# Fourteen pairs of gate-stage tiles by seven block products, convolution sums in PSUM, and low parts and weight sums on GpSimd

## The chip, the cores and the metric

The kernel runs on one core of one Trainium2 chip. The metric is the device time of one execution in microseconds (us). Engines are named as in the profile: PE is TensorE, DVE is VectorE, ACT is ScalarE, POOL is GpSimd, SP is SyncE, which issues most DMAs. On this kernel a difference of 0.2% (2.3 us) is about what a measurement tells from no change.

## The reference

One decoder layer over 1024 tokens and 1024 channels, float32 throughout.

```python
h = rmsnorm(x, ln_pre)                                  # (1024, 1024)
z = h @ w_in                                            # nine column groups
c_val, c_glu, c_gate, q, k, v, a_gate, g_conv, g_attn = split_columns(z)   # 1024 wide each, k and v 128
u  = c_val * sigmoid(c_glu)
c  = causal_depthwise_conv(u, w_dw, 31 taps) + b_dw
ya = (silu(layernorm(c)) @ w_pw * silu(c_gate)) @ w_br_conv
yb = (sliding_window_attention(q, k, v, sinks) * silu(a_gate)) @ w_br_attn
m  = sigmoid(g_conv) * ya + sigmoid(g_attn) * yb
x  = x + rmsnorm(m @ w_out, ln_post)
x  = x + sigmoid(x @ w_ple_gate) * (p @ w_ple_proj)
```

## The kernel before

Everything is kept transposed: 128 channels on the partitions, 1024 tokens along the free axis. A **tile** is 128 output channels for all 1024 tokens. It is 48 matmuls of 128x512: eight blocks of input channels, two halves of the tokens, and three passes, because a float32 product is made from values split in a rounded high part and the remainder: high x high, low weight x high input, high weight x low input. The rounded parts (`_hi`) are made by ACT, the remainders (`_lo`) by DVE, for the input once and for each tile's weights in turn (`high`, L1089, and `low`, L1558). The weights have two slots; a tile's weights can be split only when the tile two before it is done. PSUM has two slots of 1024 columns for tiles (`psg`) and four banks of 512 columns more (`psb`).

The program is one written-out order on each engine, tied by semaphores. It begins with the projection of `p` (eight short tiles), while DVE and ACT norm and split `h`. Then come 32 **gate-stage tiles** (`A0` to 31), four per round: GLU gate, value, `g_conv`, `g_attn` of the same 128 channels. `first_pair` (L653) holds the first two, `pairs(A0 + 2, Q0, ...)` the other thirty and the tiles of k and v. ACT turns each gate into tanh (`glu_and_merge`) and sends two of them to memory, DVE multiplies value and gate into `u` (L1711). Beside it DVE runs the convolution: `conv_steps` gives out the 31 taps of a row of 128 channels one by one, alternating between two sums, `conv` and `work`, both in SBUF (L1738). `tile_low(t + 1); taps(7)` or `taps(8)` fixes how many go between two weight splits. Eight q tiles follow, with the rest of the taps and the rotary turn (`rope`) on DVE; then attention beside eight tiles, and the later stages.

Two later stages (`seventh`, L1013) already use **seven block products** (Strassen's scheme, in Winograd's form): two tiles, four input-channel blocks apart by rows of the result, are made from seven products of half size instead of eight. A product is 12 matmuls. It needs sums of weight blocks, which POOL's DMAs add up in memory early in the run (`w_sums`), and sums of input blocks. Some products are added onto another product's PSUM bank, after ACT has copied the bank out (`keep`, L1376); those copies are combined by DVE (`take`). There the order of a pair's products is `P1, P2, P6, Q5, P7, Q3, P4`.

What touches the angles of the rotary turn: DVE makes them (L1687 to L1699), ACT takes two sines (L1180, L1181), POOL finishes cosine and sine (L1064 to L1067), all during the first gate-stage tiles.

Of the kernel before, what the change touches and what calls it, by code (L numbers as in the profile page):

```python
# [17 lines left out]
F32 = mybir.dt.float32  # L18
# [31 lines left out]
A0 = 0  # L50
K_TILE, V_TILE = 32, 33
Q0 = 34
C0 = 42
D0 = 50
E0 = 58
H0 = 66
I0 = 82
TILES = 98
WTILES = 82
# [34 lines left out]
def build(nc, dram):  # L94
    with ExitStack() as ctx:
# [22 lines left out]
        u_size = (4 * (PAD + S) + 31) // 32 * 32  # L118
        u = [at(f"u{j}", [PAD + S], F32, RD + 32 * KB - u_size * (2 - j)) for j in range(2)]
# [23 lines left out]
        block_raw = at("block_raw", [7, HALF], F32, GB + 24 * KB - 192)  # L143
        s_lo = at("s_lo", [4, KP, HALF], F32R, RD)
# [51 lines left out]
        v_last = cols[:, COL_TAPS:COL_TAPS + P]  # L196
# [85 lines left out]
        end_done = sem("end_done")  # L282
        merged_spilled = [sem("merged_spilled0"), sem("merged_spilled1")]
# [25 lines left out]
        banks01 = psb[:, 0:2, :].rearrange("p b s -> p (b s)")  # L309

# [153 lines left out]

        lower_rows = (4, 5, 6, 7, 0, 1, 2, 3)
# [9 lines left out]
        def _(sp):  # L475
# [29 lines left out]
            sp.dma_start(k_raw[:].bitcast(I32), POS).then_inc(pos_loaded, 16)  # L505
# [26 lines left out]

            sp.wait_ge(ps_free[0], K_TILE // 2 + 5)
# [26 lines left out]
            def load_block(b):  # L560
# [57 lines left out]
        def _(pe):  # L618
# [167 lines left out]

            first_pair()
            pairs(A0 + 2, Q0, h_hi, h_lo)

            def turn_values(k):  # L790

                if k != 1:
                    return
                pe.wait_ge(ps_free[1], 4 + V_TILE // 2 + 1)
                for c in range(NB):
                    mm = nc.tensor.transpose(psb[:, 2 + c // 4, (c % 4) * P:(c % 4 + 1) * P], v_t[:, c * P:(c + 1) * P], ident[:])
                mm.then_inc(v_turned, 1)

            tile(Q0 // 2, 0, h_hi, h_lo)
            tile(Q0 // 2, 1, h_hi, h_lo, beside=turn_values)  # L800
            pairs(Q0 + 2, C0, h_hi, h_lo)

            def scores(p, jp):
# [3 lines left out]
                if p == 0 and jp == 0:  # L807
                    pe.wait_ge(k_dup, 128)
# [234 lines left out]
        def _(pool):  # L1043
# [15 lines left out]
            pool.wait_ge(w_hi_ready, PLE_STEPS + 2)  # L1059
# [1265 lines left out]
```

## Time and profile before

| | |
|---|---|
| median of 3 runs | 1146.57 us (1145.72 to 1146.73) |
| the profiled execution | 1147.26 us |
| its span | 1145.5 us, mean granted clock 0.999 |
| PE busy | 1139.3 us (99%) |
| DVE busy | 925.0 us (81%) |
| ACT busy | 421.8 us (37%) |
| POOL busy | 29.8 us (3%) |

The busy time of PE is no measure of its pace: a matmul of 128x512 shows 390 ns, but the next one starts before it has ended. The pace is read from the chain, from the time of a run of matmuls and their count. Busy shares of DVE are averages over stages; it is fullest in the stretch of the gate-stage tiles.

### The profile page before, as it was taken

Reading aid. Unit: us, or ns where it says so; the run is one execution under the profiler, and the core shown is the slowest. Engines: PE = TensorE matmul, PEld = TensorE weight load, DVE = VectorE, ACT = ScalarE, POOL = GpSimd, SP = SyncE. Lnnn points to the kernel's source line nnn. Section 1 sums busy time; section 2 is a strip of 40 time slices with the busy share of each in tenths; the row PEclk is TensorE's granted clock in tenths of the full one; section 3 lists DMA queues with packets and bytes.
Section 4 is the critical chain, followed back from the end, with each engine's and each line's share of the span. In section 5 each row is a group of like instructions: output and inputs, shape, how many; then the busy total and the mean of one; then the engine's idle time right before and its main releaser. Section 6 shows DMA issues by size and latency. Waiting matters only on the chain.

```text
span 1145.5 us, 16085 instructions
## 1 busy us (share of the span) xinstructions
PE 1139.3 (99%) x6208; PEld 927.8 (81%) x6208; DVE 925.0 (81%) x1087; ACT 421.8 (37%) x763; POOL 29.8 (3%) x32
## 2 busy tenths in 40 slices
PE   9999999999999999999999999999999999999998
PEld 7788888888888888877777788888888888888887
DVE  5999999999999977489888589768767967557776
ACT  6422212212112121266666343332536435444342
POOL 2012010000000000000000000000000000000000
PEclk9999999999999999999999999999999999999999
DMA  9726787421221322411111211346553753334565
GB/s 350 286 92 179 206 238 201 111 92 55 73 86 50 111 51 65 101 38 57 57 57 57 74 49 44 92 135 205 166 173 120 252 182 127 115 117 141 182 200 184
DMA packets 46053, 148.00 MB, mean 129 GB/s; under 512 B 5648, under 2 KB 6416, under 8 KB 43952
## 3 DMA queue, kind: packets, MB, share of 16 engines
q1 hardware_dynamic: 32176, 92.77, 25.5%
q10 hardware_dynamic: 11520, 37.75, 9.5%
q0 software_dynamic: 2304, 16.78, 6.1%
q8 instruction: 32, 0.52, 0.2%
q14 instruction: 21, 0.17, 0.0%
HBM read 119.37 MB, written 41.94 MB: 141 GB/s over the span
## 4 chain that ended last, share of the span: by engine, by line
PE 92%; DMA 3%; DVE 3%; ACT 1%; SPq 1%; issue 1%; DVEq 0%; ACTq 0%
PE psg L629 66%; PE psb L1013 10%; PE psg L921 6%; DMA conv<-xT 2%; PE psb L835 1%; PE psg L892 1%; PE psg L1013 1%; PE psg L682 1%; PE psg L966 1%; PE psg L853 1%; ACT probs L1237 1%; PE psg L887 1%; PE psg L653 1%; PE psg L1037 1%; SPq L496 0%
## 5 line engine op out<-in xcount | busy, mean ns | idle before, releaser
L629 PE MATMUL psg<-h_hi,w_hi 128*128 128x512 f32 x768 | 236.8, 390 | 0.0
L629 PE MATMUL psg<-h_lo,w_hi 128*128 128x512 f32 x768 | 236.5, 389 | 0.0
L629 PE MATMUL psg<-h_hi,w_lo 128*128 128x512 f32 x768 | 236.4, 389 | 0.0
L1561 DVE TENSOR_TENSOR w_lo<-w_raw,w_hi 128x1024 fp32r<-128x1024 f32 x96 | 117.5, 1224 | 86.9 <-ACT w_hi L1093 83.4
L629 PEld LDWEIGHTS psg<-h_hi,w_hi 128*128 128x128 f32 x768 | 143.8, 188 | 30.5 <-issue 0.8
L629 PEld LDWEIGHTS psg<-h_lo,w_hi 128*128 128x128 f32 x768 | 144.1, 188 | 30.0
L629 PEld LDWEIGHTS psg<-h_hi,w_lo 128*128 128x128 f32 x768 | 144.1, 188 | 29.9
L1738 DVE SCALAR_TENSOR_TENSOR conv<-u,cols,conv 128x1024 f32<-128x1024 f32 x120 | 154.3, 1286 | 0.0
L1738 DVE SCALAR_TENSOR_TENSOR work<-u,cols,work 128x1024 f32<-128x1024 f32 x112 | 145.8, 1301 | 0.0
L1093 ACT ACTIVATE w_hi<-w_raw 128x1024 fp32r<-128x1024 f32 x95 | 100.5, 1057 | 103.8 <-PE psg L629 86.4
L1013 PE MATMUL psb<-s_hi,pair_w 128*128 128x512 f32 x240 | 73.9, 389 | 0.0
L1013 PEld LDWEIGHTS psb<-s_hi,pair_w 128*128 128x128 f32 x240 | 45.0, 188 | 9.4
L1994 DVE TENSOR_TENSOR pair_w<-block_raw,pair_w 128x512 fp32r<-128x512 f32 x56 | 37.9, 686 | 17.6 <-ACT pair_w L1354 17.6
L921 PE MATMUL psg<-h_hi,w_hi 128*128 128x512 f32 x128 | 51.8, 405 | 0.0
L921 PE MATMUL psg<-h_hi,w_lo 128*128 128x512 f32 x128 | 49.9, 390 | 0.0
L921 PE MATMUL psg<-h_lo,w_hi 128*128 128x512 f32 x128 | 49.9, 390 | 0.0
L1354 ACT ACTIVATE pair_w<-block_raw 128x512 fp32r<-128x512 f32 x56 | 34.5, 626 | 41.4 <-PE psb L1013 24.5
L1013 PE MATMUL psb<-s_lo,pair_w 128*128 128x512 f32 x120 | 46.7, 389 | 0.0
L629 PE MATMUL psg<-x_hi,w_hi 128*128 128x512 f32 x120 | 46.7, 389 | 0.0
L629 PE MATMUL psg<-x_hi,w_lo 128*128 128x512 f32 x120 | 46.7, 389 | 0.0
L629 PE MATMUL psg<-x_lo,w_hi 128*128 128x512 f32 x120 | 46.7, 389 | 0.0
L1013 PE MATMUL psb<-c_hi,pair_w 128*128 128x512 f32 x144 | 44.5, 390 | 0.2 <-DVE c_lo L2072 0.2
(305 smaller groups left out, 1817.5 us busy)
## 6 DMA issues: line engine op xcount, KB each, us to landing
w_raw<-weights SPq DMA_DIRECT2D x97, 512.0 KB, 3.6
gates<-ring ACTq DMA_DIRECT2D x24, 512.0 KB, 2.7
w_sums<-w_pairs POOLq DMA_DIRECT2D x12, 1024.0 KB, 7.8
ring<-gates ACTq DMA_DIRECT2D x24, 512.0 KB, 4.4
block_raw<-w_sums SPq DMA_DIRECT2D x32, 256.0 KB, 3.1
block_raw<-w_pairs SPq DMA_DIRECT2D x24, 256.0 KB, 4.6
x_rows<-x_rows SPq DMA_DIRECT2D x8, 512.0 KB, 10.7
conv<-xT SPq DMA_DIRECT2D x8, 512.0 KB, 14.9
```

The lines of the kernel that those rows point to most:

```text
L629: mm = nc.tensor.matmul(psg[:, slot, h * HALF:(h + 1) * HALF], w[:, wslot, (wk + k) * P:(wk + k + 1) * P], r[:, k, h * HALF:(h + 1) * HALF ...
L653: mm = nc.tensor.matmul(psg[:, slot, h * HALF:(h + 1) * HALF], w[:, slot, k * P:(k + 1) * P], r[:, k, h * HALF:(h + 1) * HALF], start=(k = ...
L682: mm = nc.tensor.matmul(psg[:, slot, cols_h], w[:, slot, k * P:(k + 1) * P], r[:, k, cols_h], start=(k == 0 and n == 0), stop=(k == KT - 1 ...
L835: mm = nc.tensor.matmul(psb[out_rows, 2 * jp + par, j2 * 2 * P + first:j2 * 2 * P + first + width], qo[rows, 4 * g + 2 * jp + j2, queries] ...
L853: mm = nc.tensor.transpose(psg_banks[:, bank, first + h * HD:first + h * HD + HD], probs[g][queries, 4 * jp + h, :], ident[queries, queries])
L921: mm = nc.tensor.matmul(gate_bank(p), w[:, t % 2, k * P:(k + 1) * P], r[:, k, half], start=(k == 0 and m == 0), stop=(k == KT - 1 and m == 2))
L1013: mm = nc.tensor.matmul(bank, pair_w[:, at_w, w, k * P:(k + 1) * P], r[:, k, :], start=(not onto and k == 0 and m == 0), stop=(k == KP - 1 ...
L1093: nc.scalar.activation(w_hi[:, j % 2, :], w_raw[:, j % 2, :], ACT.Copy).then_inc(w_hi_ready, 1)
L1354: nc.scalar.activation(pair_w[:, pair_slot(b), 0, :], block_raw[:, b % 7, :], ACT.Copy).then_inc(pair_hi, 1)
L1561: nc.vector.tensor_tensor(w_lo[:, slot, :], w_raw[:, slot, :], w_hi[:, slot, :].bitcast(F32), ALU.subtract).then_inc(w_lo_ready, 1)
L1738: own.step(stt(dst, src[:, j:j + S], tap(j), dst, ALU.mult, ALU.add))
L1994: nc.vector.tensor_tensor(pair_w[:, at_w, 1, :], block_raw[:, b % 7, :], pair_w[:, at_w, 0, :].bitcast(F32), ALU.subtract).then_inc(pair_l ...
```

## The change

Of the 32 gate-stage tiles only four are left as tiles (GLU and value of channel blocks 0 and 4). The other 28 are made as 14 pairs by seven block products (`EARLY`), in the order `ORDER`, in which P6 and P7 stand next to each other. Their sums of weight blocks are made in SBUF by POOL (four per pair, `early_sum`), and so are the seven low parts (`early_low`). POOL also takes over the low parts of the tiles 1 to 3, k, v and q, the sums for the convolution's mean (`add_to_mean`) and the angles of the rotary turn, now after the gate stage. The sums of the input blocks are made by DVE out of `h` before the third tile (`early_row_sum`, `early_row_low`), their high parts by ACT. The convolution works on input rows that lie in place in `conv`; its two sums lie in `psb`, and for the last row in SBUF (`last_sums`). The additions in memory for the two later stages (`w_sums`) move from POOL's first 200 us to behind the q tiles.

```diff
+ORDER = (P1, P2, Q5, P6, P7, Q3, P4)
+EARLY = [(GLU, 1), (VAL, 1), (GCONV, 0), (GCONV, 1), (GLU, 2), (VAL, 2), (GCONV, 2), (GCONV, 3), (GLU, 3), (VAL, 3)]
+EARLY += [(GATTN, i) for i in range(PAIRS)]
+        def early_bank(s, n):
+            return psg_banks[:, {P2: 1, Q5: 2, Q3: 2}.get(n, 3 * (s % 2)), :]
 # PE
+            def early_product(s, n):
+                onto = n in (P6, P7, Q3, P4)
+                pe.wait_ge(early_split_lo, b + 1)
...
+                if onto:
+                    pe.wait_ge(early_kept, kept_at(s, {P6: P1, P7: P6, Q3: Q5, P4: P7}[n]))
+                for k in range(KP):
+                    for m, (w, r) in enumerate(((0, a_hi), (1, a_hi), (0, a_lo))):
+                        mm = nc.tensor.matmul(bank, pair_w[:, at_w, w, k * P:(k + 1) * P], r[:, k, :], ...)
             first_pair()
-            pairs(A0 + 2, Q0, h_hi, h_lo)
+            tile(1, 0, h_hi, h_lo)
+            tile(1, 1, h_hi, h_lo)
+            for s in range(len(EARLY)):
+                for n in ORDER:
+                    early_product(s, n)
...
+            tile(K_TILE // 2, 0, h_hi, h_lo)
+            tile(K_TILE // 2, 1, h_hi, h_lo)
 # POOL
+            low(1)
+            low(2)
+            low(3)
+            for s in range(len(EARLY)):
+                early_low(s, P1)
+                early_sum(s, Q5)
+                early_low(s, P2)
+                early_sum(s, P7)
+                early_low(s, Q5)
+                early_sum(s, P6)
+                early_sum(s, P4)
+                early_low(s, P6)
+                early_low(s, P7)
+                early_low(s, Q3)
+                early_low(s, P4)
+                if s in EARLY_MEANS:
+                    add_to_mean(EARLY_MEANS[s])
 # ACT
+            early_sum_high(1, 1)
+            early_sum_high(2, 2)
+            product_done(0, 0)
+            high(0, 2)
...
+            def early_keep(s, n):
+                act.wait_ge(early_made, 7 * s + PLACE[n] + 1)
...
+                nc.scalar.activation(dst, early_bank(s, n), ACT.Copy).then_inc(early_kept, 1)
...
+            for j in range(KT):
+                query_tile(j)
+                if j < KT - 1:
+                    high(Q0 // 2, j + 2)
+                if j == 1:
+                    act.wait_ge(ang_ready, 1)
+                    nc.scalar.activation(sin_t[:], cos_t[:], ACT.Sin)
+                    nc.scalar.activation(ring[:, 1, :], cos_t[:], ACT.Sin, scale=0.5).then_inc(sin_ready, 1)
 # DVE
-            for t in range(2, Q0 - 1):
-                if t % 4 == 2:
-                    conv_input(t // 4)
-                tile_low(t + 1)
-                taps(7 if t % 2 == 0 else 8)
+                    for shift in range(3, TAPS):
+                        dst = sums_of[shift % 2][:, shift:]
+                        own.step(stt(dst, row[:, 0:S - shift], tap(shift), dst, ALU.mult, ALU.add))
...
+            plain_input(0)
+            taps(11)
+            plain_input(1)
+            for s, (kind, i) in enumerate(EARLY):
+                for n in ORDER:
+                    if n == Q5:
+                        early_take(s, 0)
+                    if n == Q3:
+                        early_take(s, 1)
+                        early_take(s, 2)
+                    if n == P4 and kind == VAL:
+                        early_take(s, 3)
+                    if n == Q5:
+                        taps(1 if kind == VAL else 2)
+                    elif n == Q3:
+                        taps(0 if kind == VAL else 1)
+                    else:
+                        taps(2)
```

Three places show how the order moves. The first is ACT from the last high part of `h` to the gate of the first tile, before:

```order
L1093 ACTIVATE w_hi<-w_raw 128x1024 [waits w_loaded0,tile_done,ps_free1]
L1161 ACTIVATE tanh_t<-psg 128x1024
L1093 ACTIVATE w_hi<-w_raw 128x1024 [waits tile_done,w_loaded1]
L1166 ACTIVATE ring<-psg 128x1024 [waits tile_done]
L1107 DMA gates<-ring 128x1024 [waits ps_free0]
```

and with the change, where L1335 is `high`, L1400 the high parts of the input sums and L1422 those of a product's weights:

```order
L1400 ACTIVATE early_hi<-conv 128x2048 [waits early_s_made] x2
L1335 ACTIVATE w_hi<-w_raw 128x1024 [waits tile_done,w_loaded0]
L1406 ACTIVATE tanh_t<-psg 128x1024
L1335 ACTIVATE w_hi<-w_raw 128x1024 [waits tile_done,w_loaded1]
L1400 ACTIVATE early_hi<-conv 128x2048 [waits early_s_made] x2
L1412 ACTIVATE tanh_t<-psg 128x1024 [waits ps_free1,tile_done]
L1422 ACTIVATE pair_w<-early_raw 128x512 [waits early_loaded0,tile_done] x2
```

Two high parts of sums now stand ahead of the high part of the third tile's weights. The second place is PE, from the P6 of a pair to its P7, with the change (L927 is `early_product`; before, plain tiles of L629 stood here, with no wait inside a tile):

```order
L927 MATMUL psg<-early_hi,pair_w 128x512 [waits early_kept,early_s_ready,early_split_lo]
L927 MATMUL psg<-early_hi,pair_w 128x512
L927 MATMUL psg<-early_lo,pair_w 128x512
L927 MATMUL psg<-early_hi,pair_w 128x512 x2
L927 MATMUL psg<-early_lo,pair_w 128x512
L927 MATMUL psg<-early_hi,pair_w 128x512 x2
L927 MATMUL psg<-early_lo,pair_w 128x512
L927 MATMUL psg<-early_hi,pair_w 128x512 x2
L927 MATMUL psg<-early_lo,pair_w 128x512
L927 MATMUL psg<-early_hi,pair_w 128x512 [waits early_kept,early_s_ready,early_split_lo]
```

The last row is the first matmul of P7; its `early_kept` is the copy of the very product that stands above it. The third place is POOL at the q tiles. Before, the first rows of the same work stood by themselves, long before the q tiles:

```order
L1064 TENSOR_TENSOR cos_t<-v_t 128x1024 [waits sin_ready]
L1066 TENSOR_SCALAR cos_t<-cos_t 128x1024 [waits pool_own]
L1067 TENSOR_SCALAR sin_t<-sin_t,cols 128x1024
L1074 DMA w_sums<-w_pairs 128x2048
L1076 DMA w_sums<-w_pairs 128x2048 [waits sums_made]
```

With the change (L1222 is `low` of a tile; the first one here is that of the second q tile, the five in one row begin with that of the third q tile):

```order
L1222 TENSOR_TENSOR w_lo<-w_raw,w_hi 128x1024 [waits w_lo_ready,w_hi_ready]
L1289 TENSOR_SCALAR ring<-sin_t 128x1024 [waits pool_own]
L1291 TENSOR_TENSOR cos_t<-cos_t,ring 128x1024 [waits pool_own]
L1293 TENSOR_SCALAR cos_t<-cos_t 128x1024 [waits pool_own]
L1251 TENSOR_TENSOR sums<-sums,conv 128x1024 [waits csum_done,conv_done]
L1296 TENSOR_TENSOR cos_t<-ring 128x1024 [waits sin_ready]
L1298 TENSOR_SCALAR cos_t<-cos_t 128x1024 [waits pool_own]
L1299 TENSOR_SCALAR sin_t<-sin_t,cols 128x1024
L1222 TENSOR_TENSOR w_lo<-w_raw,w_hi 128x1024 [waits w_lo_ready,w_hi_ready] x5
```

The wait for the sines and the three instructions behind it now stand ahead of the low part of the third q tile's weights.

## Rows read from the trace of the kernel before

**Rows 1.** The page: busy us (share of the span) and instructions of each engine.
```profile
PE 1139.3 (99%) x6208; PEld 927.8 (81%) x6208; DVE 925.0 (81%) x1087; ACT 421.8 (37%) x763; POOL 29.8 (3%) x32
```

**Rows 2.** The chain in order of time: start us, us, what.
```profile
54.05 360.40 PE psg L629 x1590
...
812.71 59.85 PE psb L1013 x264
```

**Rows 3.** Windows of the gate stage: us, then busy us and count per engine.
```profile
54.00:380.00 326.00, 326.00 (x1440) 269.95 (x1439) 311.30 (x268) 65.98 (x62) 20.39 (x19) 1.00 0.43 125
```

**Rows 4.** Timeline around a copied product: start us, us, engine, line, operation.
```profile
815.27 0.61 PE L1013 MATMUL psb<-c_hi,pair_w 128*128 128x512 f32 x2
815.47 0.60 ACT L1376 ACTIVATE kept<-psb 128x512 f32<-128x512 f32 x1 [0.28 <-PE psb L1013]
```

**Rows 5.** Timeline where PE waits for an ACT copy, and POOL's one low part.
```profile
27.30 1.00 ACT L1123 ACTIVATE ple_out<-psb 128x1024 f32<-128x1024 f32 x1
27.57 2.38 POOL L1061 TENSOR_TENSOR w_lo<-w_raw,w_hi 128x1024 fp32r<-128x1024 f32 x1 [2.88 <-DVE w_lo L1561]
28.08 1.28 DVE L1664 SCALAR_TENSOR_TENSOR conv<-conv,cols,psb 128x1024 f32<-128x1024 f32 x1 [0.65 <-DMA conv<-xT]
28.36 0.73 PE L736 MATMUL psb<-p_hi,wp_hi 128*128 128x512 f32 x2 [0.59 <-ACT ple_out L1123]
28.93 0.63 PE L736 MATMUL psb<-p_hi,wp_lo 128*128 128x512 f32 x2
```

**Rows 6.** Timeline of the third tile's start: DVE and PE.
```profile
49.32 0.17 DVE L1684 TENSOR_SCALAR half_b<-cols 128x8 f32<-128x8 f32 x1
53.89 0.61 PE L629 MATMUL psg<-h_hi,w_hi 128*128 128x512 f32 x2
```

**Rows 7.** Two dependent sums of 128x2048 on DVE, and their splits (groups by form).
```profile
786.92 4.69 DVE L2005 TENSOR_TENSOR conv<-conv 128x2048 f32<-128x2048 f32 x2
L1363 ACT ACTIVATE s_hi<-conv 128x2048 fp32r<-128x2048 f32 x4 | 7.5, 1906 | 0.8 <-PE psg L966 0.8
L2010 DVE SCALAR_TENSOR_TENSOR s_lo<-conv,s_hi 128x2048 fp32r<-128x2048 f32 x4 | 9.1, 2287 | 1.6 <-ACT s_hi L1363 1.6
```

**Rows 8.** Timeline of a tile's read-out, the way to POOL's cosine, DVE beside.
```profile
75.85 1.03 ACT L1173 ACTIVATE ring<-psg 128x1024 f32<-128x1024 f32 x1 [8.26 <-PE psg L629]
77.69 1.06 ACT L1093 ACTIVATE w_hi<-w_raw 128x1024 fp32r<-128x1024 f32 x1 [0.82 <-ACT ring L1173]
82.15 2.53 POOL L1064 TENSOR_TENSOR cos_t<-v_t 128x1024 f32<-128x1024 f32 x1 [52.20 <-ACT v_t L1181]
82.85 2.91 DVE L1738 SCALAR_TENSOR_TENSOR work<-u,cols,work 128x1024 f32<-128x1024 f32 x1
84.78 1.90 POOL L1066 TENSOR_SCALAR cos_t<-cos_t 128x1024 f32<-128x1024 f32 x1
86.67 3.80 POOL L1067 TENSOR_SCALAR sin_t<-sin_t,cols 128x1024 f32<-128x1024 f32 x1
98.04 1.27 DVE L1738 SCALAR_TENSOR_TENSOR conv<-u,cols,conv 128x1024 f32<-128x1024 f32 x1
99.24 1.27 DVE L1738 SCALAR_TENSOR_TENSOR work<-u,cols,work 128x1024 f32<-128x1024 f32 x1
```

**Rows 9.** Group by form: a DVE operation that reads and writes PSUM, 128x512.
```profile
L1816 DVE COPY_PREDICATED psb<-upper_q,psb 128x512 f32<-128x512 uint32 x28 | 19.3, 689 | 1.1
```

**Rows 10.** Timeline of PE's first matmuls.
```profile
1.27 5.49 PE L754 MATMUL psb<-ones 128*128 128x128 f32 x24 [1.27 <-DVE ones L1624]
6.41 1.12 PE L736 MATMUL psg<-p_hi,wp_hi 128*128 128x512 f32 x2
7.37 0.39 PE L736 MATMUL psb<-p_hi,wp_hi 128*128 128x512 f32 x1
```

**Rows 11.** DMA issues: count, KB each, median us to landing.
```profile
w_raw<-weights SPq DMA_DIRECT2D x97, 512.0 KB, 3.6
gates<-ring ACTq DMA_DIRECT2D x24, 512.0 KB, 2.7
```

More of the change, by code:

```diff
@@ L47 @@
 TWO_PI = (6.28125, 0.0019350051879882812, 3.0199159819567e-07)
[L50 to L59, printed above, removed]
+K_TILE, V_TILE = 4, 5
+Q0 = 6
+C0 = 14
+D0 = 22
+E0 = 30
+H0 = 38
+I0 = 54
+TILES = 70
+WTILES = 54
 PAIRS = KT // 2
@@ new lines, in _ @@
+            own.wait()
+            own.step(nc.gpsimd.tensor_scalar(sin_t[:], sin_t[:], MAGIC, None, ALU.subtract))
+            low(Q0)
+            for part in TWO_PI:
+                if part == TWO_PI[2]:
+                    low(Q0 + 1)
+                own.wait()
+                own.step(nc.gpsimd.tensor_scalar(angle, sin_t[:], -part, None, ALU.mult))
+                own.wait()
+                own.step(nc.gpsimd.tensor_tensor(cos_t[:], cos_t[:], angle, ALU.add))
+            own.wait()
@@ new lines, in early_tanh_of @@
+            def early_tanh_of(s, n):
+                row, half = early_quarter(n)
+                place = ring[:, row, half]
+                if n == 3:
+                    act.wait_ge(early_made, 7 * s + PLACE[P4] + 1)
+                    ring_free(act, s, row)
+                    source = early_bank(s, P4)
+                else:
+                    act.wait_ge(early_read, early_read_by(s, n))
+                    source = place
+                nc.scalar.activation(place, source, ACT.Tanh, scale=0.5).then_inc(early_tanh, 1)
@@ new lines, in early_spill, with early_events @@
+            def early_spill(s, row):
+                kind, i = EARLY[s]
+                act.wait_ge(early_tanh, 4 * TANHS[s] + 4)
+                spill(GATES[:, i + KP * row + (2 * KT if kind == GCONV else 0), :], row)
+            def early_events(s, n):
+                if n in (P1, Q5, P6, P7):
+                    early_keep(s, n)
+                if s in TANHS:
+                    if n == P6:
+                        early_tanh_of(s, 0)
+                    if n == P4:
+                        early_tanh_of(s, 1)
+                        early_tanh_of(s, 2)
+                        early_tanh_of(s, 3)
+                if n == P4 and s in SPILLS:
+                    early_spill(s, 0)
+                    early_spill(s, 1)
@@ new lines, in _ @@
+            for b in range(6):
+                early_high(b)
+            for b in range(6, EARLY_PRODUCTS):
+                for s, n in early_made_since(b):
+                    early_events(s, n)
+                early_high(b)
+                if b == EARLY_LAST + 4:
+                    high(K_TILE // 2 - 1, 2)
+            for c in range(early_slot_before(EARLY_PRODUCTS - 1) + 1, EARLY_PRODUCTS):
+                early_events(c // 7, ORDER[c % 7])
+            act.wait_ge(w_loaded[1], (V_TILE // 2 + 1) * 16)
@@ L1745, in _ @@
+                    yield
             steps = conv_steps()
@@ L1901, in _ @@
                     tile_low(C0 + p // 2 + 1)
+                if p > 1 and p % 2 == 0:
+                    taps(2)
                 if p == 4:
@@ L1910, in _ @@
                 if p == 14:
+                    taps(TAPS)
                     dve.wait_ge(sums_hi_ready, 1)
```

408 lines of the change are left out of this document (289 added, 119 removed).

## The prediction, made before the changed kernel was run

> **What bounds the kernel now.** I read the page's busy shares first, then the chain of waits, then windows and timelines of the stages that the change touches. PE is busy for 99% of the span [rows 1], and in the chain in order of time 1590 matmuls of the gate stage and of k, v and q follow one another in 360.40 us without another engine between them [rows 2]. So PE sets the end, and its pace is 360.40 / 1590 = 0.2267 us for a matmul of 128x512. A tile (48) is 10.88 us. The later stage with block products runs at the same pace: 59.85 / 264 = 0.2267 us [rows 2]. A product (12) is 2.72 us. What saves matmuls saves time one for one, and every wait that PE newly gets is paid in full. Second, DVE is nearly as full in this stage: 311.3 of 326 us [rows 3], 95%. POOL is nearly empty (20.4 us of the same window).
>
> **Matmuls removed.** A pair of tiles costs 96 matmuls, by seven products 84. Fourteen pairs save 14 x 12 = 168, at 0.2267 us: **-38.1 us**. That is exact as long as products follow without a gap.
>
> **They don't: P7 behind P6.** Both are added onto one bank, and P7 waits for ACT's copy of P6, the product just before it. (The other copies have a product or more in between: P1 for P6, Q5 for Q3, P7 for P4.) In the old stage a copy starts at 815.47 where the next product had begun at 815.27, 0.20 us earlier, and lasts 0.60 us [rows 4]. PE starts 0.06 us after an ACT copy that it waits for (27.30 + 1.00 = 28.30, start 28.36), and the first two matmuls after such a wait take 28.93 - 28.36 = 0.57 us where two take 0.45 [rows 5]: 0.12 more. Sum 0.98 us, per pair, 14 times: **+13.7 us** (12.6 if the restart is cheaper, 16.8 if ACT is sometimes found busy and it is 1.2). A pair then lasts 7 x 2.72 + 0.98 = 20.0 us, against 21.8 before.
>
> **Do DVE and POOL keep up with 20.0 us?** A tap starts every 99.24 - 98.04 = 1.20 us [rows 8]. A pair of gates has 13 taps and 3 combinations of products (0.69 each, taken from the nearest 128x512 row, which also reads and writes PSUM [rows 9]): 15.6 + 2.1 = 17.7 us. A value pair has 11 taps, 3 combinations and 4 multiplications: 13.2 + 4.8 = 18.0 us. The low parts of weights are off DVE. POOL's low part of 128x1024 took 2.38 us [rows 5]; halved, 1.19 us, and 11 per pair are 13.1 us, with four times a sum of 2.5 us for the mean. It would set the pace from 20.0 / 11 = 1.82 us on. Lags in between are covered: a product's weights may be split once the product six back is done, so five products (13.6 us) hide ACT's 0.6 and POOL's queue of two or three operations. I cost all this at nothing, with 0 to 13 us kept for it (POOL's operation at 1.9 us: 11 x 1.9 - 20.0 = 0.9 us, 14 times).
>
> What these two do to each other is in the rows. POOL's 82.15 to 84.68 lay over a tap that began at 82.85 and took 2.91 us instead of 1.27 [rows 8]: it waited for POOL. That tap read two tensors in SBUF. The operation at 28.08 read one in SBUF and one in PSUM beside POOL's 27.57 to 29.95 and took 1.28 us [rows 5], its usual time. The new taps have their sums in PSUM, so I let them run beside POOL. The Trainium skill says the same (SBUF — State Buffer, Who interferes with whom: a DVE instruction with two SBUF inputs and a GpSimd one that reads SBUF exclude each other, one with a single SBUF input doesn't contend); both rows agree. It also says that issue order decides who blocks, which bears on the next two terms, where DVE again reads two SBUF tensors.
>
> **The third tile starts late.** DVE's small operations end at 49.49 and the third tile began at 53.89 [rows 6]. Now ACT makes two high parts of input sums before it comes to this tile's weights. The second sum is ready at 49.49 + 4.69 = 54.2 (two dependent sums took 4.69), its high part takes 1.91 [rows 7]: 56.1; the weights' high part 1.06 [rows 8]: 57.2. Then POOL's low part, 2.38. But DVE's fourth sum, with two SBUF inputs, runs from 56.5 to 58.9. If it excludes POOL, the low part ends at 61.3, otherwise at 59.6. With 0.06 to PE: 7.4 or 5.8 us after 53.89. I take the rows' exclusion: **+7.4 us**.
>
> **The fourth tile.** It needs slot 1, which DVE frees after four low parts of sums (2.29 each [rows 7]) and one multiplication (1.2). From 61.3, with POOL's low part for this tile (2.4) pushed in between: 61.3 + 9.2 + 2.4 + 1.2 = 74.1, wanted at 61.3 + 10.9 = 72.2: **+1.9 us** (0 to 3).
>
> **The third q tile.** POOL comes to its low part only behind the sines and three operations, and ACT comes to the sines only behind the read-out of the second q tile. With t the time when the third q tile could start: read-out from t + 0.20 [rows 4] for 1.0 us [rows 8]; from ACT's high part through the load of the sine table and two sines to POOL's start 82.15 - 77.69 = 4.46 us; POOL's three operations 82.15 to 86.67 + 3.80 = 90.47, 8.3 us, beside the same kind of taps as here (the last row's sums lie in SBUF) [rows 8]; the low part 2.4. Together 16.4 us. All of this lay beside running tiles before; now nothing covers it: **+16.4 us**. Without any hindrance from DVE POOL's three are 2.5 + 1.9 + 1.9 and the wait is 14.3; with one more blocking, 18.
>
> Up to there POOL is just in time. From the last product's end T: three tanh and the spill (2.7 [rows 11]) T + 5.4, positions loaded (3.6) T + 9.0, four operations of 1.9 T + 16.6, first q tile's low part T + 19.0, wanted at T + 21.8; four more operations and the second's T + 30.3, wanted at T + 32.6. Margins of 2.8 and 2.3 us: 0, with 5 us kept at the high end.
>
> **PE's clock.** The granted clock reads 1.00 throughout and PE has no idle stretch of such a length after it has started, so no row shows what a wait of 7 or 16 us does. The nearest are the first matmuls: those at 6.41 are half as fast (7.37 - 6.41 = 0.96 us for two) as later, 6.1 us after PE began at 1.27 [rows 10]. At most each of the two long waits costs half of 6.1 us, 3.05; at least nothing. I take the middle, 1.5 each: **+3.0 us** (0 to 6.1). The Trainium skill speaks against this change here (TensorE: Matmul & The Clock Gate, Part 1 and Why this matters for your kernels): the array's default is the lower of its two levels, 1.2 GHz, and idling between bursts brings it back there. By that rule the term is not zero; no run here shows it yet.
>
> **Attention.** Taps are gone by then, but POOL brings two sums for the mean and the additions in memory beside a DVE that is short of time, with SBUF inputs on both: **+1.0 us** (-1 to +5). The additions are needed hundreds of microseconds later. The rotary turn and its packing wait for q tiles, as before.
>
> **The sum.** -38.1 + 13.7 + 7.4 + 1.9 + 16.4 + 3.0 + 1.0 = +5.3 us. On the profiled execution (1147.26 us; the span is 1145.5) that is 1152.6; the median of the runs lies 0.7 us below this execution: **1152 us**. Bounds: -38.1 + 12.6 + 5.8 + 14.3 - 1 = -6.4, or 1140; and -38.1 + 16.8 + 7.4 + 3 + 18 + 6.1 + 5 + 5 = +23.2, or 1170.
>
> **Rivals.**
> *The third q tile doesn't wait.* If POOL's chain of sines were ready by the end of the second q tile, or its low part came first, the sum loses 16.4 and one restart (1.5): 1134 us, faster. It decides at the end of the second q tile: from the point where POOL has passed its three operations by then, which asks for ACT's sines some 14 us (more than a tile) sooner. For it: the angles themselves are ready at about T + 37, before ACT is. Against: ACT's order puts the sines behind that read-out, POOL's puts three operations ahead of five low parts.
> *All waits at their short end.* No exclusion at the third tile, none at the q tile, no clock loss: -38.1 + 13.7 + 5.8 + 14.3 = -4.3, 1142 us; half of that way is no change.
> *DVE or POOL sets the pace of the pairs.* From 1.82 us for POOL's 128x512, or 1.38 us for a tap in PSUM. At 1.9 us for POOL +12.6, so 1165; at 1.5 us for a tap 13 x 1.5 + 2.1 = 21.6, 1.6 us over, 14 times: 1174. If taps in PSUM excluded POOL as those in SBUF do, a pair would take 17.7 + 13.1 = 30.8 us and the run about 1300. Against: the rows at 28.08 and of 0.69 us.
> That a seven-product pair saves less than 12 matmuls is excluded by the equal pace.
>
> **Chances.** The forecast with its waits 0.60 (1149 to 1162); all waits short 0.22, most of it within 0.2%; no wait at the third q tile 0.08; DVE or POOL as pace 0.10. The range from 1141 to 1167 leaves out the 1134 and the far end of the last. 0.2% is 2.3 us, what a measurement can tell here. Faster by more: 0.08 and a third of the short waits, with something for what I overlook, 0.17. Within: 0.20. Slower: 0.63.
>
> **What would show it.** In the timeline of the changed kernel: PE idle for about 1 us before each P7, released by ACT's copy of P6, and nowhere else inside a pair; a pair every 20.0 us; an idle of 6 to 7 us before the third tile and 14 to 18 before the third q tile, both released by POOL's low part; matmuls at half pace right behind them; POOL's 128x512 near 1.2 us and taps at 1.2 us whatever POOL does. An interval of pairs above 20.5 us or a missing wait at the third q tile would make it wrong.

## The result, and the profile after

The changed kernel takes 1155.99 us (median of 4 runs, 1154.67 to 1158.57) against 1146.14 us before: ratio 1.0088, 95% interval 1.0070 to 1.0107, 9.9 us slower. The forecast was 1152 us, range 1141 to 1167, slower at 0.63. The profiled execution took 1154.67 us with a span of 1152.9; it is the fastest of the four. Against the profiled execution before (1147.26) it is 7.4 us slower, and these 7.4 are what the two profiles can account for. The other 2.5 of the 9.9 stand in no profile.

The page's first part answers [rows 1]: 168 matmuls fewer on PE, 30.2 us less of its busy time, POOL now busy for a quarter of the span.

```profile
PE 1109.1 (96%) x6040; PEld 898.0 (78%) x6040; DVE 946.6 (82%) x1092; ACT 482.8 (42%) x909; POOL 316.3 (27%) x218
```

The span grew by 7.4 us, so PE's idle time grew by 37.6. The waits of PE over the whole span (what waits, what released it: us in total, times, longest us) name it:

```profile
PE psg L740 <- POOL w_lo L1222: 23.5, 2, 16.0
PE psg L927 <- ACT kept L1434: 10.9, 14, 0.8
PE psb L992 <- DMA qo<-pack: 4.0, 1, 4.0
PE psb L865 <- DVE ones L1923: 1.3, 1, 1.3
```

The first three are new, the fourth stood there before. L740 is the tile's matmul, L927 a product's, L992 the scores of attention; the releaser `qo<-pack` is the transfer of the turned queries from `pack` to `qo`. The chain in order of time, where [rows 2] had one row of 1590 matmuls, is now cut at each pair (a row starts with P7 and ends with the next pair's P6):

```profile
54.78 4.49 POOL w_lo L1222
59.30 23.78 PE psg L740 x96
83.08 10.89 PE psg L927 x48
94.74 19.34 PE psg L927 x84
114.84 19.34 PE psg L927 x84
...
356.05 8.44 PE psg L927 x36
364.50 24.48 PE psg L740 x108
389.85 19.08 PE psg L740 x84
418.25 3.77 POOL sin_t L1299
424.89 12.74 PE psg L740 x48
446.77 30.88 DVE last_sums L2037 x19
484.05 3.32 DVE pack L2110
490.47 5.30 DMA qo<-pack
...
820.12 59.85 PE psb L1170 x264
```

Pairs come every 114.84 - 94.74 = 20.10 us. The copy in front of P7, in the timeline of PE:

```profile
94.74 0.69 PE L927 MATMUL psg<-early_hi,pair_w 128*128 128x512 f32 x2 [0.78 <-ACT kept L1434]
```

The third tile's start, in the timelines of PE and DVE:

```profile
47.13 7.08 DVE L1992 TENSOR_TENSOR conv<-conv 128x2048 f32<-128x2048 f32 x3
54.74 2.29 DVE L1992 TENSOR_TENSOR conv<-conv 128x2048 f32<-128x2048 f32 x1 [0.54 <-DVE conv L1992]
59.30 1.22 PE L740 MATMUL psg<-h_hi,w_hi 128*128 128x512 f32 x2 [7.52 <-POOL w_lo L1222]
```

DVE's fourth sum of input blocks begins at 54.74, POOL's low part at 54.78 (the first row of the chain), and the low part takes 4.49 us. The last row of the chain answers the one at 812.71 of [rows 2]: everything before it is 7.4 us late, what follows takes as long as before.

The timeline of PE and POOL at the third q tile (start us, us, engine, line, operation, and in brackets the idle before it and its releaser):

```profile
414.38 1.89 POOL L1296 TENSOR_TENSOR cos_t<-ring 128x1024 f32<-128x1024 f32 x1 [10.64 <-ACT ring L1511]
416.36 1.89 POOL L1298 TENSOR_SCALAR cos_t<-cos_t 128x1024 f32<-128x1024 f32 x1
418.24 3.79 POOL L1299 TENSOR_SCALAR sin_t<-sin_t,cols 128x1024 f32<-128x1024 f32 x1
422.00 6.06 POOL L1222 TENSOR_TENSOR w_lo<-w_raw,w_hi 128x1024 fp32r<-128x1024 f32 x2
...
424.89 1.22 PE L740 MATMUL psg<-h_hi,w_hi 128*128 128x512 f32 x2 [15.97 <-POOL w_lo L1222]
425.91 1.05 PE L740 MATMUL psg<-h_hi,w_lo 128*128 128x512 f32 x2
426.76 1.05 PE L740 MATMUL psg<-h_lo,w_hi 128*128 128x512 f32 x2
427.62 0.90 PE L740 MATMUL psg<-h_hi,w_hi 128*128 128x512 f32 x2
428.35 0.63 PE L740 MATMUL psg<-h_hi,w_lo 128*128 128x512 f32 x2
```

The steps are those that [rows 8] had beside running tiles, and PE now waits for all of them. Behind the wait two matmuls start 0.85 us apart instead of 0.45. Windows of PE in the idle, just behind it and later (us, busy and count, granted clock, DMA share, GB/s):

```profile
409.50:424.50 15.00, 0.00 (x0) 0.55 0.00 0
425.00:428.00 3.00, 3.00 (x7) 0.50 0.71 206
429.50:434.50 5.00, 5.00 (x23) 1.00 0.23 88
```

A granted clock of 0.50 is the lower of the two levels, 1.2 GHz. The timeline of DVE, cut to the last row's taps, whose sums lie in SBUF, and the second rotary turn's last operation:

```profile
412.04 18.27 DVE L2037 SCALAR_TENSOR_TENSOR last_sums<-conv,cols,last_sums 128x1021 f32<-128x1021 f32 x9
...
446.69 30.95 DVE L2037 SCALAR_TENSOR_TENSOR last_sums<-conv,cols,last_sums 128x1012 f32<-128x1012 f32 x19
...
484.05 3.31 DVE L2110 TENSOR_TENSOR pack<-pack,rtmp 96x1024 f32<-96x1024 f32 x1
```

These taps take 18.27 / 9 = 2.03 and 30.95 / 19 = 1.63 us where one alone takes 1.20 [rows 8]. Behind them stands the second rotary turn, and attention waits for its result.

### The profile page after: what moved, and what is told of

It reads as the page before. It is cut to its first block, busy times and chain, and to the rows that moved or that the text cites. A ratio compares the mean times of both kernels' runs of the same rounds, so it can differ in the third digit from the quotient of the medians.

```text
span 1152.9 us, 16104 instructions
## 1 busy us (share of the span) xinstructions
PE 1109.1 (96%) x6040; PEld 898.0 (78%) x6040; DVE 946.6 (82%) x1092; ACT 482.8 (42%) x909; POOL 316.3 (27%) x218
## 3 DMA queue, kind: packets, MB, share of 16 engines
q1 hardware_dynamic: 35648, 92.77, 23.9%
## 4 chain that ended last, share of the span: by engine, by line
PE 83%; DVE 8%; DMA 3%; ACT 2%; POOL 1%; issue 1%; SPq 1%; DVEq 0%; ACTq 0%; POOLq 0%
PE psg L740 35%; PE psg L927 23%; PE psb L1170 10%; PE psg L1078 6%; DVE last_sums L2037 3%; PE psb L992 1%; PE psg L1049 1%; PE psg L1170 1%; DMA conv<-xT 1%; DMA x_rows<-x_rows 1%; PE psg L793 1%; PE psg L1123 1%; PE psg L1010 1%; ACT kept L1434 1%; PE psg L1044 1%
## 5 line engine op out<-in xcount | busy, mean ns | idle before, releaser
L2037 DVE SCALAR_TENSOR_TENSOR psb<-conv,cols,psb 128x1021 f32<-128x1021 f32 (+6 forms) x196 | 232.9, 1265 | 0.0
L927 PE MATMUL psg<-early_hi,pair_w 128*128 128x512 f32 x448 | 139.4, 392 | 10.9 <-ACT kept L1434 10.9
L1229 POOL TENSOR_TENSOR pair_w<-early_raw,pair_w 128x512 fp32r<-128x512 f32 x91 | 125.2, 1381 | 62.0 <-ACT pair_w L1422 61.7
L740 PE MATMUL psg<-h_hi,w_hi 128*128 128x512 f32 x320 | 101.0, 397 | 23.5 <-POOL w_lo L1222 23.5
L927 PEld LDWEIGHTS psg<-early_hi,pair_w 128*128 128x128 f32 x448 | 83.0, 188 | 33.1 <-POOL pair_w L1229 15.2
L927 PE MATMUL psg<-h_hi,pair_w 128*128 128x512 f32 x336 | 103.5, 389 | 0.0
L740 PE MATMUL psg<-h_hi,w_lo 128*128 128x512 f32 x320 | 99.5, 392 | 0.0
L740 PE MATMUL psg<-h_lo,w_hi 128*128 128x512 f32 x320 | 99.4, 392 | 0.0
L740 PEld LDWEIGHTS psg<-h_hi,w_hi 128*128 128x128 f32 x320 | 60.6, 191 | 37.5 <-issue 17.2
L927 PE MATMUL psg<-early_lo,pair_w 128*128 128x512 f32 x224 | 87.4, 390 | 0.0
L1335 ACT ACTIVATE w_hi<-w_raw 128x1024 fp32r<-128x1024 f32 x66 | 69.6, 1054 | 37.0 <-PE psg L740 34.6
L1422 ACT ACTIVATE pair_w<-early_raw 128x512 fp32r<-128x512 f32 x91 | 56.8, 628 | 57.8 <-PE psg L927 45.5
L927 PEld LDWEIGHTS psg<-h_hi,pair_w 128*128 128x128 f32 x336 | 63.1, 188 | 13.2
L740 PEld LDWEIGHTS psg<-h_hi,w_lo 128*128 128x128 f32 x320 | 60.9, 190 | 13.0
L740 PEld LDWEIGHTS psg<-h_lo,w_hi 128*128 128x128 f32 x320 | 60.6, 189 | 12.7
L927 PE MATMUL psg<-h_lo,pair_w 128*128 128x512 f32 x168 | 65.4, 389 | 0.0
L1222 POOL TENSOR_TENSOR w_lo<-w_raw,w_hi 128x1024 fp32r<-128x1024 f32 x13 | 38.3, 2949 | 70.0 <-ACT w_hi L1335 66.9
```

The source lines that it names most:

```text
L740: mm = nc.tensor.matmul(psg[:, slot, h * HALF:(h + 1) * HALF], w[:, wslot, (wk + k) * P:(wk + k + 1) * P], r[:, k, h * HALF:(h + 1) * HALF ...
L927: mm = nc.tensor.matmul(bank, pair_w[:, at_w, w, k * P:(k + 1) * P], r[:, k, :], start=(not onto and k == 0 and m == 0), stop=(k == KP - 1 ...
L1222: nc.gpsimd.tensor_tensor(w_lo[:, t % 2, :], raw, w_hi[:, t % 2, :].bitcast(F32), ALU.subtract).then_inc(w_lo_ready, 1)
L1229: nc.gpsimd.tensor_tensor(pair_w[:, at_w, 1, :], early_source(s, n), pair_w[:, at_w, 0, :].bitcast(F32), ALU.subtract).then_inc(early_spli ...
L1335: nc.scalar.activation(w_hi[:, j % 2, :], w_raw[:, j % 2, :], ACT.Copy).then_inc(w_hi_ready, 1)
L1422: nc.scalar.activation(pair_w[:, early_slot(b), 0, :], early_source(s, n), ACT.Copy).then_inc(early_split_hi, 1)
```

## The experiments

All are edits of the changed kernel (1155.99 us); the diffs show the lines that matter, with `...` where others are left out. The line numbers of the rows shift by a few with each edit. Times are medians, rows come from one profiled execution. A difference between two rows can therefore miss that between two medians by about 2 us: the profiled execution of experiment 2 is 2.4 us above its median, that of experiment 5 is 2.5 above.

**1. P6 ahead of Q5.** PE and what follows it use an order of their own, `RUN`; the weights are still made in `ORDER`.

```diff
+RUN = (P1, P2, P6, Q5, P7, Q3, P4)
...
-            return 4 * s + {P1: 1, Q5: 2, P6: 3, P7: 4}[n]
+            return 4 * s + {P1: 1, P6: 2, Q5: 3, P7: 4}[n]
...
-                for n in ORDER:
+                for n in RUN:
                     early_product(s, n)
```

> Only the order in which PE runs the seven products of a pair changes: P1, P2, P6, Q5, P7, Q3, P4 in place of P1, P2, Q5, P6, P7, Q3, P4; weights are made in the old order. Theory A (the 1.05 us that each pair of 20.10 us has above 84 x 0.2267 = 19.05 us is ACT's copy of P6 that P7 waits for): no product stands behind the one whose copy it needs, the 14 idles go, pairs come every 19.05 us, -14.7 us, 1141 us (1140 to 1143; a remainder of up to 2 us is left for the last pair, whose products have three weight slots instead of six). Rival B (the copy hides a second limit: DVE, busy for 259.1 of the 282 us of the pairs, 18.5 us for each, or POOL, 14.8 us for each): pairs come every 19.4 to 19.7 us, other waits of PE stand in the pairs, released by DVE or by POOL's low parts, 1146 to 1150 us. Rival C (the idle moves to another product): 1154 to 1157 us.

Measured 1144.44 us (ratio to the kernel before 0.9985, 0.9976 to 0.9994). The chain holds the pairs in two rows:

```profile
83.25 258.58 PE psg L933 x1140
344.91 5.73 PE psg L933 x24
350.64 24.48 PE psg L746 x108
```

258.58 / 1140 = 0.2268 us a matmul, no gap, and one idle of 0.37 in the last pair. The pairs end 364.50 - 350.64 = 13.9 us earlier: theory A. DVE was no second limit. Only 11.5 us reach the end, so the time lies above the range that I had: 0.9 stay at the third q tile (16.9 instead of 16.0, since POOL's first operation behind the sines took 2.85 us), 0.3 at attention's start (4.3 instead of 4.0), and from there to the late products 325.2 us pass instead of 324.1.

**2. Low parts before the sines.**

```diff
             add_to_mean(4)
+            low(Q0 + 2)
+            low(Q0 + 3)
             pool.wait_ge(sin_ready, 1)
...
-            for t in range(Q0 + 2, C0 - 1):
+            for t in range(Q0 + 4, C0 - 1):
```

> POOL makes the low parts of the third and fourth q tile's weights before it waits for ACT's sines, not behind the three operations that follow the sines. Theory A (the third q tile waits 16.0 us for nothing but that place in POOL's order, and what follows is bound by DVE): this idle goes and with it the slow matmuls behind it (about 1.8 us), but DVE has the taps of the last row to do before the rotary turn whatever PE does: its turn can start 11.5 us sooner (it was idle for 11.47 us at 430.3 us), not 17.8, so the start of attention waits about 10 us instead of 4.0. Net -11.5 us, 1144.5 us (1143 to 1147). Rival B (DVE isn't what the start of attention waits for): the whole 17.8 us stays, 1138 us. Rival C (another operation holds the third q tile as long, ACT's read-out or POOL's backlog): an idle of over 8 us stays there, 1149 to 1156 us.

Measured 1148.64 us (ratio 1.0019, 1.0009 to 1.0029), -7.4, which is 1.6 us above theory A's range. The third q tile starts without a wait, as theory A says, and the wait comes back at attention, 13.2 us where I had about 10. The first of PE's waits:

```profile
PE psb L992 <- DMA qo<-pack: 13.2, 1, 13.2
```

DVE now works through from the pairs to attention: its taps still take 28.82 / 19 = 1.52 us beside POOL, and it ends the second turn at 480.6, only 6.8 us sooner than in the changed kernel (487.4). So more than half of the 16.0 + 1.7 us couldn't be won by this edit alone: behind them stood DVE.

**3. The third tile's high part first.**

```diff
+            product_done(0, 0)
+            high(0, 2)
+            nc.scalar.activation(tanh_t[:], psg[:, 0, :], ...).then_inc(ps_free[0], 1)
             early_sum_high(1, 1)
             early_sum_high(2, 2)
-            product_done(0, 0)
-            high(0, 2)
-            nc.scalar.activation(tanh_t[:], psg[:, 0, :], ...).then_inc(ps_free[0], 1)
```

> ACT makes the high part of the third tile's weights and its tanh before the high parts of the first two input sums, not behind them. Theory A (behind the third tile's wait of 7.5 us lies a longer one of the fourth tile, whose slot DVE frees only behind four sums and four low parts, at 71.5 us): the third tile starts at about 52 us, the fourth waits about 9 us until 71.6, the first product of the pairs starts at 82 to 84 us as before (83.08). 1155.5 us (1154 to 1157). Rival B (ACT's order alone makes the loss at this place, as my sum had it with 7.4 + 1.9 us): the third tile's wait goes, the fourth waits 0 to 3 us, -6 to -9 us, 1147 to 1150 us.

Measured 1157.16 us: nothing won. The third tile doesn't wait, the fourth does:

```profile
71.72 1.19 PE L740 MATMUL psg<-h_hi,w_hi 128*128 128x512 f32 x2 [8.63 <-DVE conv L2010]
```

Theory A: 7.5 us at one place and 8.6 at the next are one loss, set by DVE's sums of input blocks.

**4. The last row's sums in PSUM.**

```diff
-            if q == KT - 1:
-                return last_sums[n][:]
             return psb[:, 2 * n:2 * n + 2, :]...
...
-                    pe.wait_ge(conv_done, KT - 1)
+                    pe.wait_ge(conv_done, KT)
```

> The convolution's sums of the last row lie in PSUM, as those of the other seven rows, not in SBUF; attention waits for all eight rows instead of seven, whose taps are done before the rotary turn anyway. Theory A (a tap with two SBUF inputs and a POOL operation with SBUF inputs exclude each other, one with a PSUM input doesn't): nine taps beside POOL's sines take 1.2 us each, not 18.27 / 9 = 2.0, and the nineteen later ones 1.2, not 30.95 / 19 = 1.63; POOL's three operations behind the sines take 1.9 + 1.9 + 1.9 us, not 1.89 + 1.89 + 3.79, so the third q tile waits 14 us, not 16.0; the second rotary turn is done about 8 us earlier and the wait of 4.0 us at the start of attention goes with its slow matmuls (about 1.3 us). Sum -7 us, 1149 us (1148 to 1151). Rival B (POOL and DVE slow each other down whatever memory the sums are in): taps stay at 1.6 to 2.0 us, 1155 to 1157 us.

Measured 1151.04 us (ratio 1.0043, 1.0029 to 1.0057), -5.0. DVE's taps and POOL's operations at the same place:

```profile
414.09 10.74 DVE L2035 SCALAR_TENSOR_TENSOR psb<-conv,cols,psb 128x1021 f32<-128x1021 f32 x9
446.58 22.32 DVE L2035 SCALAR_TENSOR_TENSOR psb<-conv,cols,psb 128x1012 f32<-128x1012 f32 x19
```

```profile
415.39 1.89 POOL L1294 TENSOR_TENSOR cos_t<-ring 128x1024 f32<-128x1024 f32 x1 [10.75 <-ACT ring L1509]
417.37 1.04 POOL L1296 TENSOR_SCALAR cos_t<-cos_t 128x1024 f32<-128x1024 f32 x1
418.39 2.84 POOL L1297 TENSOR_SCALAR sin_t<-sin_t,cols 128x1024 f32<-128x1024 f32 x1
```

Nine taps take 1.19 us each and nineteen 1.17, whatever POOL does. POOL's second and third operation take 1.04 and 2.84 us instead of 1.89 and 3.79; the first stays at 1.89. Attention starts without a wait, the third q tile waits 13.8. That is theory A. The missing 2 us are a wait of 1.8 for DVE inside attention, where two operations of 0.69 us each took 3.78 together beside POOL's last sum for the mean.

**5. Only two low parts of sums ahead of the fourth tile's multiplication.** ACT makes the third tile's high part first, as in experiment 3; its lines, and those of two waits that go with the new order, are left out here.

```diff
-            for made, n in enumerate((1, 2, 0, 3)):
-                early_row_low(n, made + 1)
+            early_row_low(2, 1)
+            early_row_low(0, 2)
...
             plain_input(0)
-            taps(11)
+            early_row_low(1, 3)
+            early_row_low(3, 4)
+            taps(8)
             plain_input(1)
+            taps(3)
```

> As in the run before, ACT makes the third tile's high part first; besides, the multiplication that frees the fourth tile's slot stands on DVE behind the low parts of two input sums (those whose rows it overwrites), not of all four, and three of the eleven taps between the first two multiplications go behind the second. Theory A (the fourth tile waits for DVE's chain of sums, whatever ACT does): DVE reaches the multiplication two low parts sooner, at 66 instead of 71.7 us, the fourth tile waits 3 to 4 us instead of 8.6, the first product of the pairs starts at about 78 us instead of 83.08, -5 us, 1151 us (1149 to 1153). Rival B (DVE's work is only put off, and the third product of the first pair waits for the second multiplication instead): the pairs start sooner but a wait of 3 to 6 us stands in the first pair, 1154 to 1157 us.

Measured 1152.95 us (ratio 1.0056, 1.0043 to 1.0070), -3.0. The fourth tile waits 4.3 us instead of 8.6. Theory A; the multiplication ran at 66.93, since POOL's two low parts each cost DVE about 2 us there (three sums took 9.08, two low parts 6.68; without POOL in experiment 10 they took 7.08 and 4.49).

**6. The wait filled with matmuls.**

```diff
+            pe.wait_ge(ps_free[0], Q0 // 2 + 5)
+            for _ in range(56):
+                nc.tensor.matmul(psg[:, 0, 0:HALF], ones[:], h_hi[:, 0, 0:HALF], start=True, stop=True)
             pairs(Q0 + 2, C0, h_hi, h_lo)
```

> While PE waits for the third q tile's weights it runs 56 matmuls of 128x512 (12.7 us) on ones and h into the bank that the tile clears afterwards; nothing else changes. Theory A (the seven slow matmuls behind that wait are the price of the idle itself): the tile starts at about 424.9 us as before, its 48 matmuls take 10.9 to 11.3 us instead of 12.74, -1.7 us, 1154.3 us. Rival B (they are slow because POOL, DVE or DMA disturb them): 12.7 us as before, 1156 us. Rival C (the filler is in the way: it ends after the weights are ready): the tile starts 1 to 3 us later, 1156 to 1158 us.

Measured 1159.70 us, slower than any theory had it. A wait of 3.3 us was left, and the matmuls behind it were as slow as behind 16.0. And 4.1 us of a new wait appeared at a later q tile:

```profile
458.56 14.13 DVE L2040 SCALAR_TENSOR_TENSOR last_sums<-conv,cols,last_sums 128x1005 f32<-128x1005 f32 x12
...
462.16 12.73 POOL L1225 TENSOR_TENSOR w_lo<-w_raw,w_hi 128x1024 fp32r<-128x1024 f32 x1 [8.13 <-ACT w_hi L1338]
...
475.02 1.22 PE L740 MATMUL psg<-h_hi,w_hi 128*128 128x512 f32 x2 [4.13 <-POOL w_lo L1225]
```

A POOL operation of 2.4 us took 12.73 while DVE gave out taps on SBUF without a pause, at 14.13 / 12 = 1.18 us each, undisturbed. In the changed kernel's rows above both got slower; here DVE kept POOL out. The 3.7 us more than in the changed kernel are, about, the 4.1, 2.5 of slow matmuls behind them, a wait of 2.0 inside attention and 0.6 by which the third q tile starts later (425.48 against 424.89), less the wait of 4.0 at attention's start with its 1.5 of slow matmuls, which is gone.

**7. The filler again, with the last row in PSUM** (edits 4 and 6).

> The 56 matmuls in the wait for the third q tile again, now with the last row's sums in PSUM. Theory A (in the run with the filler alone, POOL's low part of 12.73 us was locked out by taps that read two tensors in SBUF, and it cost 4.1 us of idle; the slow matmuls come because the rest of the wait was 3.3 us long): with sums in PSUM POOL's low parts take 2.4 us each throughout, the rest of the wait is 13.8 - 12.7 = 1.1 us, the matmuls behind it run at full pace, as they do behind the 0.8 us idles of the pairs: 1151.0 - 1.7 = 1149.3 us. Rival B (any stop longer than those of the pairs brings the slow matmuls): 1151.0 us. Rival C (POOL's low part is held up by something other than SBUF inputs, for instance by DVE working without a pause in whatever memory): a low part of over 5 us shows again, 1154 to 1160 us.

Measured 1148.75 us against 1151.04 of edit 4 alone. The rest of the wait is 1.1 us and the clock stays up:

```profile
423.22 0.72 PE L738 MATMUL psg<-h_hi,w_hi 128*128 128x512 f32 x2 [1.12 <-POOL w_lo L1223]
423.78 0.62 PE L738 MATMUL psg<-h_hi,w_lo 128*128 128x512 f32 x2
```

POOL's low parts of the later q tiles take 2.39 to 2.41 us. Theory A on both points.

**8. Edits 1, 2 and 4 together.**

> Three edits together: P6 ahead of Q5, low parts of the third and fourth q tile ahead of the sines, the last row's sums in PSUM. Theory A (each wait is gone for its own reason and DVE, once its taps no longer exclude POOL, arrives in time): pairs every 19.05 to 19.1 us (-14.0), no idle at the third q tile and none at the start of attention (-16.0 - 4.0 and about -3.3 of slow matmuls), +1.8 for the wait that attention got from DVE when the last row lay in PSUM: 1156.0 - 14.0 - 16.0 - 4.0 - 3.3 + 1.8 = 1120.5 us (1118 to 1124). Rival B (DVE, busy for over 93% of the pairs and of what follows, is now the bound up to attention): the start of attention waits 5 us or more for the rotary turn, 1125 to 1132 us.

Measured 1120.97 us (ratio 0.9779, 0.9766 to 0.9793): theory A. Alone the three gave 11.5 + 7.4 + 5.0 = 23.9 us, together 35.0. The wait of 13.2 us at attention that edit 2 alone had is gone, since with edit 4 DVE is there in time.

**9. Edits 1, 2, 4 and 5.**

> The three edits and, with them, the third tile's high part first and the fourth tile's multiplication behind two low parts of sums. Theory A (the loss at the third and fourth tile is independent of the others): -5 us on top, 1115.5 us (1113 to 1120). Rival B (DVE has no slack left up to attention, and what PE gains at the third tile it waits out before attention or inside the pairs): as with three edits, within 1.5 us.

Measured 1117.92 us (ratio 0.9757): 3.05 more, what edit 5 gave alone. Theory A in kind, 2 us short in size as there.

**10. Two edits more: the third and fourth tile's low parts on DVE, a mean sum later.**

```diff
-            low(2)
-            low(3)
...
                 early_row_sum(n, made)
+                if made in (0, 3):
+                    tile_low((2, 0, 0, 3)[made])
...
             low(C0)
-            add_to_mean(6)
...
                     if made == 4:
+                        add_to_mean(KT - 2)
                         add_to_mean(KT - 1)
```

> The version with four edits and two more: DVE makes the low parts of the third and fourth tile's weights, not POOL, and POOL adds the seventh row to the mean later, beside attention. Theory A (each of POOL's two low parts costs DVE 2.2 us of its chain of sums, 9.09 us for three sums where 7.08 were seen; on DVE they cost 1.2 each; and POOL's mean sum of 3.37 us held DVE's rotary operations of 3.07 and 3.41 us ahead of attention, from which its wait of 1.93 us comes): the fourth tile waits 2.3 us instead of 4.3, attention's wait for DVE goes: 1117.9 - 2.0 - 1.9 = 1114.0 us (1112.5 to 1116). Rival B (DVE loses as much by the work as it gains by the missing exclusion): the fourth tile waits 4 to 5 us, and only the 1.9 us at attention are won, 1116 us.

Measured 1117.81 us: no gain, and 1.8 us above theory A's range. The first half did as theory A said: the fourth tile waits 2.6 us, attention starts 2.8 us sooner. The second lost it again: the two mean sums fell on DVE operations for which PE waits.

```profile
470.62 5.15 POOL L1255 TENSOR_TENSOR sums<-sums,conv 128x1024 f32<-128x1024 f32 x2
...
473.60 3.32 DVE L2188 TENSOR_TENSOR probs<-probs,rden 128x512 f32<-128x512 f32 x2
...
476.98 1.12 PE L1014 MATMUL psg<-ident,probs 64*128 64x64 f32 x16 [3.30 <-DVE probs L2188]
```

**11. The two mean sums much later** (`made == 4` becomes `made == 12`).

> The version with six edits, with POOL's two sums for the mean put off further, from the fourth to the twelfth of its steps in memory (from 470 to about 542 us). Theory A (the 3.3 us that PE waits for DVE in the first steps of attention is POOL's 5.15 us for these two sums, which stretched DVE's operations to 2.10 and 3.32 us at a place where PE waits for them; later DVE has room): this wait goes, with some of the slow matmuls behind it, and none takes its place: 1117.8 - 3.3 - 1 = 1113.5 us (1112 to 1115.5). Rival B (attention waits for DVE there anyway, or wherever the sums fall they delay PE as much): a wait of 2 to 4 us for DVE stands in attention, 1116 to 1118 us.

Measured 1114.94 us (ratio 0.9724, 0.9711 to 0.9738): theory A. The wait is down to 0.2 us. This version is 31 us faster than the kernel before and 41 faster than the changed one.

## Why the prediction was right

The forecast lay 4 us under the measurement. The side, the pace of products, the waits at P7, at the third tile and at the third q tile, and what released them came out as written. By its own steps, each against the two profiled spans:

| step | forecast | measured |
|---|---|---|
| matmuls removed | -38.1 | -38.1 (experiment 1: 0.2268 us each over 1140) |
| P7 behind P6 | +13.7 | 14 x (20.10 - 19.05) = +14.7 |
| third tile | +7.4 | +5.4 (59.30 against 53.89; the wait is 7.5, since the first two tiles ended 2.2 sooner) |
| fourth tile | +1.9 | 0 |
| third q tile | +16.4 | +16.0 |
| clock | +3.0 | +1.9, +1.7 and, at attention, +1.5 |
| start of attention | 0 | +4.0 |
| attention | +1.0 | 0 besides the clock |

The right column gives -38.1 + 14.7 + 5.4 + 16.0 + 5.1 + 4.0 = +7.1, against 7.4 of the spans.

That the sum came so close is in part luck. The forecast had 5.3 us too much (3.9 at the third and fourth tile, 0.4 at the third q tile, 1.0 in attention) and 7.1 too little (1.0 at P7, 2.1 for the clock, 4.0 at the start of attention), and the two nearly cancel. The largest single miss is the last, a wait that the forecast had at nothing.

**P7 behind P6** was right in mechanism and 1.05 instead of 0.98 us in size: PE starts 0.14 us behind the copy (which runs from 94.00 for 0.60), not 0.06. Experiment 1 showed that nothing stood behind it.

**DVE and POOL keep up.** POOL's sums of 128x512 took 1.29 us where I had 1.19 by halving, its low parts 1.38 in the mean, both far from 1.82. Taps with sums in PSUM kept their 1.2 us beside 207.6 us of POOL's work in the 282 us of the pairs. The combination `kept_q5 - kept`, with two SBUF inputs, took 1339 ns in the mean of 11, where those with one input in PSUM took 692; PE waited for none of them.

**The third tile.** The exclusion was there: POOL's low part took 4.49 us, and I had 4.1 (57.2 to 61.3). But DVE's small operations ended 2.3 us sooner than in the kernel before (47.2, not 49.5), and all that hangs on them came sooner: 5.4 us instead of 7.4. That the wait itself reads 7.5 is chance, since the tiles ahead of it ended sooner too. The load of `conv` from `xT` on which the chain waits there landed 2.3 us sooner (43.07 against 45.34); why, no experiment asked. Also, the sum priced this wait and the fourth tile's as two, and experiment 3 showed one loss under both: ACT's order could be mended without winning anything.

**The third q tile** was within 0.4 us. One reading in it was wrong: I took POOL's last two operations as 1.9 us each without DVE in the way, and experiment 4 shows 1.04 and 2.84. What the prediction did not say is that this wait hid DVE's lateness: with it gone alone, only 7.4 us were won (experiment 2), and the rest needed experiment 4's edit. Its rival "The third q tile doesn't wait" took the whole 16.4 + 1.5 us as gain and was too hopeful by some 10.

**The step that failed** is "The rotary turn and its packing wait for q tiles, as before." It put the start of attention at nothing, and the runs show a wait of 4.0 us. In the kernel before, DVE had slack ahead of attention, busy for 35.3 of 60 us (window in us, then busy us and count of PE, its weight loads, DVE, ACT and POOL):

```profile
430.00:490.00 60.00, 60.00 (x266) 49.48 (x264) 35.30 (x33) 10.25 (x11) 0.00 (x0) 1.00 0.33 79
```

Now the second turn stands behind nineteen taps in SBUF that POOL stretches to 1.63 us, and one of its own operations took 3.31. I had applied the exclusion to POOL's operations, at two places, and nowhere to DVE's. With 1.20 us a tap the nineteen would end 8 us sooner, and in experiment 4, where they took 1.17, there was no wait. By the Trainium skill (SBUF — State Buffer, Who interferes with whom) a DVE instruction with two SBUF inputs and a GpSimd one that reads SBUF exclude each other while one with a single SBUF input does not contend: experiment 4, 1.19 us against 2.03, agrees.

**The clock** term was put in the middle of 0 and 3.05 for each long wait. Counted over the first forty matmuls behind an idle (time taken less 40 x 0.2267), the loss was 1.86 us behind 7.5, 1.69 behind 16.0, 1.65 behind 8.6 (experiment 3), 1.73 behind 3.3 (experiment 6) and 1.7 behind 2.6 (experiments 10 and 11). It was 1.56 behind 16.9 in experiment 1 and 2.76 behind 13.8 in experiment 4, so it scatters and doesn't grow with the wait. Behind 0.78 (each pair) and 1.1 us (experiment 7) it was 0.1, the restart alone. So the third wait, of 4.0 us, cost nearly as much as the two that I had. By the Trainium skill (TensorE: Matmul & The Clock Gate, Part 1) idling between bursts brings the array back to its lower level; the 0.55 in the wait and the 0.50 behind it agree.

## What to carry to other kernels

When work moves to an engine that shares memory with another, price the sharing on both engines and along the whole stretch: here the same taps cost 1.2 or up to 2.0 us by where their sums lay. A wait that is about to be removed is worth only as much as the next engine can keep up with; lay the chain of the second-busiest engine beside it before counting the gain. Put a product between a copy and the product that needs it: that order alone was worth 11.5 us.

## What the hardware showed that I had not expected

- DVE can keep POOL out for far longer than one operation: 12.73 us for one of 2.4 (experiment 6), while in the changed kernel the same low part, also beside a run of such taps, took 2.60. It began at 461.53 there and at 462.16 in experiment 6. Perhaps the moment at which the two meet decides; no experiment shows it. PE waited 4.1 us for it.
- PE's matmuls are slow behind a wait of 2.6 us (granted clock 0.53 in the 3 us behind it, experiment 11) as behind one of 16, at 1.6 to 2.8 us each, and not behind one of 1.1.
- POOL's operations of one input differ by what they do: with a factor and a sum in one, 1.04 us at 128x1024; with a single factor per partition 2.84 (the rows of experiment 4).
